# The skip term inside the Toeplitz kernel, a gate unit cut in two, and nine modulation tiles loaded ahead of the Toeplitz matrix

## The reference

```python
mod = c_silu @ w_ada + b_ada                    # six vectors of 1024: sh1 sc1 ga1 sh2 sc2 ga2
h = modulate(x, g_mix, sh1, sc1); proj = h @ w_in
u_a, z_b, gate_logits = ...                     # widths 512, 2*512 (after gelu), 2*1024
y = u * d_skip                                  # s5_mixer: the skip term
for direction in range(2):                      # complex scans over ctx, then over x
    y = y + orient(s5_readout(s5_scan(...)))
y_a = gelu(y) * sigmoid(gelu(y) @ w_glu + b_glu)
y_b = sgu_mixer(z_b, ...)
g_a, g_b = split(sigmoid(gate_logits + b_gate))
x = x + ga1 * ((g_a * (y_a @ w_proj_a) + g_b * (y_b @ w_proj_b)) @ w_out)
h2 = modulate(x, g_ffn, sh2, sc2)
x = x + ga2 * conv_ffn(h2, ...)                 # the second half of the time
```

## Time and profile before

| | |
|---|---|
| median of 3 runs | 466.66 us (465.65 to 468.84) |
| the profiled execution | 465.06 us |
| its span | 463.2 us |
| granted TensorE clock | 0.999 |
| PE busy | 447.6 us (97%) |
| DVE busy | 401.2 us (87%) |
| ACT busy | 116.5 us (25%) |
| POOL busy | 45.3 us (10%) |
| moved by DMA | 98.47 MB |

### The profile page before, as it was taken

How to read it: one execution, slowest core, us unless ns; L and a number is a source line. 1 busy time by engine, 2 the same in 40 slices (tenths; PEclk the granted TensorE clock), 3 DMA queues, 4 the chain that set the end, 5 groups by cost and what they waited for, 6 DMA issues and landing times.

```text
span 463.2 us, 7678 instructions
## 1 busy us (share of the span) xinstructions
PE 447.6 (97%) x2637; PEld 345.0 (74%) x2637; DVE 401.2 (87%) x818; ACT 116.5 (25%) x216; POOL 45.3 (10%) x73
## 2 busy tenths in 40 slices
PE   8999999989999998999999999999999999999994
PEld 5677857888888886785478888888888887444453
DVE  3599999999999867969836999999999999899744
ACT  5423355135104023201152222122122122200002
POOL 2001100002104222000000111011011011000000
PEclk9999999999999999999999999999999999999999
DMA  8994499943999999989069554554554354400002
GB/s 300 418 420 162 130 347 87 299 161 72 109 219 411 419 392 399 416 342 398 3 253 405 206 190 148 209 226 162 200 201 150 147 181 70 158 0 0 1 0 91
DMA packets 24604, 98.47 MB, mean 213 GB/s; under 512 B 7608, under 2 KB 9280, under 8 KB 16128
## 3 DMA queue, kind: packets, MB, share of 16 engines
q1 hardware_dynamic: 14592, 72.34, 44.8%
q0 software_dynamic: 5056, 18.61, 12.9%
q10 hardware_dynamic: 4928, 7.14, 4.2%
HBM read 95.49 MB, written 2.60 MB: 212 GB/s over the span
## 4 chain that ended last, share of the span: by engine, by line
PE 59%; DVE 20%; DMA 16%; POOL 2%; ACT 1%; issue 1%; DVEq 0%; SPq 0%; ACTq 0%; POOLq 0%
PE bank L756 33%; PE bank L767 14%; DVE s_region L1052 11%; DMA h_all<-mod_w 9%; PE bank L711 5%; DMA s_region<-k_scratch 5%; PE bank L667 5%; DVE s_region L1171 2%; DMA ctx_region<-ctx_t 2%; DVE s_region L1309 1%; DVE h_all L1225 1%; POOL s_region L373 1%; PE bank L482 1%; POOL s_region L383 1%; DMA k_scratch<-s_region 1%
## 5 line engine op out<-in xcount | busy, mean ns | idle before, releaser
L756 PE MATMUL bank<-h_all,s_region 128*128 128x256 f32 x704 | 152.3, 379 | 0.2 <-ACT h_all L966 0.2
L756 PEld LDWEIGHTS bank<-h_all,s_region 128*128 128x128 f32 x704 | 133.2, 190 | 19.1 <-ACT h_all L966 0.6
L1571 DVE SCALAR_TENSOR_TENSOR ctx_region<-ctx_region,pk_sb 128x189 f32<-128x189 f32 (+2 forms) x352 | 130.2, 443 | 0.3 <-DVE ctx_region L1571 0.2
L573 PE MATMUL bank<-h_all,ring_region 128*128 128x256 f32 x256 | 56.2, 380 | 0.3 <-DVE s_region L1340 0.3
L573 PEld LDWEIGHTS bank<-h_all,ring_region 128*128 128x128 f32 x256 | 48.4, 190 | 7.4 <-DVE s_region L1340 0.5
L767 PE MATMUL bank<-s_region,ring_region 128*128 128x512 f32 (+1 forms) x132 | 47.8, 522 | 0.0
L767 PEld LDWEIGHTS bank<-s_region,ring_region 128*128 128x128 f32 x132 | 25.0, 190 | 22.5 <-issue 20.3
L984 ACT ACTIVATE ctx_region<-bank 128x512 f32<-128x512 f32 x22 | 13.1, 597 | 113.3 <-PE bank L756 60.1
L1052 DVE TENSOR_TENSOR s_region<-s_region,power 128x2048 f32<-128x2048 f32 (+1 forms) x16 | 38.1, 2420 | 0.2
L396 POOL TENSOR_TENSOR ring_region<-gates,ctx_region 128x256 f32 x22 | 17.2, 784 | 178.2 <-ACT gates L992 178.2
L482 PE MATMUL bank<-h_all,ring_region 128*128 128x256 f32 x128 | 31.1, 388 | 0.2 <-ACT h_all L829 0.2
(11 more groups left out here) (242 smaller groups left out, 529.5 us busy)
## 6 DMA issues: line engine op xcount, KB each, us to landing
s_region<-up_w SPq DMA_DIRECT2D x33, 1024.0 KB, 4.9
ring_region<-ring_w SPq DMA_DIRECT2D x20, 1024.0 KB, 9.0
s_region<-mod_w POOLq DMA_DIRECT2D x20, 512.0 KB, 15.4
s_region<-early_w SPq DMA_DIRECT2D x4, 1024.0 KB, 21.8
s_region<-out_w SPq DMA_DIRECT2D x4, 1024.0 KB, 12.7
gates<-mod_w ACTq DMA_DIRECT2D x8, 512.0 KB, 5.4
gates<-early_w SPq DMA_DIRECT2D x2, 1024.0 KB, 10.8
s_region<-k_scratch POOLq DMA_DIRECT2D x8, 256.0 KB, 12.4
```

The lines of the kernel that those rows point to most:

```text
L573: mx = pe.matmul(bank[5 - j % 2][:, mm * TOK:(mm + 1) * TOK], ring[:, u % RING, (mm * KD + k) * P:(mm * KD + k + 1) * P], h_x[:, k, :], st ...
L756: mx = pe.matmul(bank[s % 3][:, half * TOK:(half + 1) * TOK], up_ring[:, s, (half * KD + k) * P:(half * KD + k + 1) * P], h2[:, k, :], sta ...
L1571: dve.scalar_tensor_tensor(out=o, in0=a, scalar=cw[:, tile[half], (dy + 1) * 3 + dx + 1], in1=o, op0=ALU.mult, op1=ALU.add).then_inc(s_con ...
```

## The change

- **Skip term.** `eye_h`, an identity of 16 by 16 repeated down the partitions, comes in with the packed parameters. DVE multiplies it by `s5_d` once (`skip_eye`, 128x64), and adds it to lag 0 of K in `k_sb` between the copies of jobs 5 and 7. The copy `u_x` (L1270) and the eight multiply-adds of L1434 are gone. ACT takes the gelu straight from the two PSUM banks, in two instructions. ACT copies job 6 before it stores K, and the store waits for the addition (`s_k_skip`).
- **POOL's queue.** `c_bc` and tiles 0 to 8 are issued as soon as their buffers are free; then come the wait for the stored K and the eight loads of `m_toep`, then tiles 9 to 23.
- **Modulation sums.** DVE makes 9 instead of 12 ahead of ga1's addition and 14 in all ahead of `y_a`, where there were 18; then three, one behind each of the merges 0 to 5, and sum 23 behind the sums of the output weights.
- **Gate unit 0** is cut in two: its first half stands where it stood, its second between chunk jobs 1 and 2.
- **Merge.** One multiplication of 128x512 stands for two of 128x256.

```diff
@@ packed parameters
-("s5_d", KS), ("conv_b", 2 * KF), ("conv_w", 2 * KF * 9)]:
+("s5_d", KS), ("conv_b", 2 * KF), ("conv_w", 2 * KF * 9), ("eye_h", H)]:
+        skip_eye = a_raw[:, 0:KS * H].rearrange("p (m h) -> p m h", m=KS)
+        k_lag0 = k_sb.rearrange("p (m j h) -> p m j h", m=KS, j=LAGS)[:, :, T - 1, :]
@@ POOL's queue
-            pool.wait_ge(s_k_out, 16)
-            for tau in range(T):
-                pool.dma_start(m_toep[tau * H:(tau + 1) * H, :, :],
-                               k_dram[:, :, (T - 1 - tau) * H:(2 * T - 1 - tau) * H].rearrange("m (g h) n -> h (m g) n", h=H)).then_inc(s_m, 16)
             pool.wait_ge(s_e_ps, 8)
-            pool.wait_ge(s_m, 16 * T)
             pool.dma_start(c_bc, c_row.partition_broadcast(P)).then_inc(s_crow, 16)
             for t in range(MT):
                 if t == S5_TILES:
                     pool.wait_ge(s_sgu_ps, 2)
+                if t == MTS:
+                    pool.wait_ge(s_k_out, 16)
+                    for tau in range(T):
+                        pool.dma_start(m_toep[tau * H:(tau + 1) * H, :, :],
+                                       k_dram[:, :, (T - 1 - tau) * H:(2 * T - 1 - tau) * H].rearrange("m (g h) n -> h (m g) n", h=H)).then_inc(s_m, 16)
                 if t >= MTS:
                     pool.wait_ge(s_mt_used, t - MTS + 1)
@@ PE
-            def gate_unit(j):
+            def gate_unit(j, halves=(0, 1)):
-                for mm in range(2):
+                for mm in halves:
-                mx.then_inc(s_unit, 1)
+                if halves[-1] == 1:
+                    mx.then_inc(s_unit, 1)
             pe.wait_ge(s_win, 16)
-            gate_unit(0)
+            gate_unit(0, (0,))
             pe.wait_ge(s_uchunk, 16 * T)
             pe.wait_ge(s_z, 2)
             for job in range(E_BANKS):
+                if job == 2:
+                    gate_unit(0, (1,))
...
-            pe.wait_ge(s_ygelu, 1)
+            pe.wait_ge(s_ygelu, 2)
...
-            pe.wait_ge(s_y, 2 * KS)
             projection(3, 0)
@@ ACT
-            act.wait_ge(s_ux, 1)
+            act.wait_ge(s_u_out, 16 * KS)
...
-            act.wait_ge(s_k, 2)
+            chunk_inputs_copied(6)
+            act.wait_ge(s_k_skip, 1)
             act.dma_start(k_dram[:].rearrange("m p n -> p m n"), k_sb[:, :].rearrange("p (m n) -> p m n", m=KS)).then_inc(s_k_out, 16)
-            chunk_inputs_copied(6)
...
-            act.wait_ge(s_y, 2 * KS)
-            act.activation(y_gelu.rearrange("p m (c t) -> p m t c", t=T), y_feat, ACT.Gelu_apprx_tanh).then_inc(s_ygelu, 1)
+            for b in range(2):
+                act.wait_ge(s_y_tr, b + 1)
+                act.activation(y_gelu.rearrange("p m (c t) -> p t m c", t=T)[:, 4 * b:4 * b + 4],
+                               bank[b][:, :].rearrange("p (t m c) -> p t m c", t=4, m=KS), ACT.Gelu_apprx_tanh).then_inc(s_ygelu, 1)
@@ DVE
-            dve.wait_ge(s_uf, KS)
-            dve.tensor_copy(u_x[:, :].rearrange("p (m c) -> p m c", c=CH), u_feat.rearrange("p m t c -> p (m t) c")[:, :, CH:2 * CH]).then_inc(s_ux, 1)
+            dve.wait_ge(s_pk2, 16)
+            tt(skip_eye, par("eye_h").unsqueeze(1).broadcast_to([P, KS, H]), par("s5_d").unsqueeze(2).broadcast_to([P, KS, H]), ALU.mult)
...
             for job in (3, 4, 5, 7):
+                if job == 7:
+                    dve.wait_ge(s_k, 2)
+                    dve.tensor_tensor(k_lag0, k_lag0, skip_eye, ALU.add).then_inc(s_k_skip, 1)
                 dve.wait_ge(s_e_ps, job + 1)
...
-            modulation_sums(0, 12)
-            dve.wait_ge(s_mt_used, 12)
+            modulation_sums(0, 9)
+            dve.wait_ge(s_mt_used, 9)
             dve.tensor_tensor(mod2[:, 0:KD], mod_sum[:, 0:KD], par("b_ada")[:, 2 * KD:3 * KD], ALU.add).then_inc(s_ga1, 1)
-            dve.wait_ge(s_pk2, 16)
-            for b in range(2):
-                dve.wait_ge(s_y_tr, b + 1)
-                y_ps = bank[b][:, :].rearrange("p (t m c) -> p m t c", t=4, m=KS)
-                for m in range(KS):
-                    dve.scalar_tensor_tensor(out=y_feat[:, m, 4 * b:4 * b + 4], in0=u_x[:, m * TOK:(m + 1) * TOK].rearrange("p (t c) -> p t c", t=T)[:, 4 * b:4 * b + 4],
-                                             scalar=par("s5_d")[:, m:m + 1], in1=y_ps[:, m], op0=ALU.mult, op1=ALU.add).then_inc(s_y, 1)
-            modulation_sums(12, 18)
+            modulation_sums(9, 14)
             for m in range(KS):
                 dve.wait_ge(s_glu, m + 1)
                 dve.tensor_tensor(y_a[:, m, :], y_gelu[:, m, :], glu_gate[:, m, :], ALU.mult).then_inc(s_ya, 1)
-            modulation_sums(18, 20)
+            modulation_sums(14, 17)
...
-                t = merge_tmp[:, 0, :], merge_tmp[:, 1, :]
-                tt(t[0], src[:, 0:TOK], gates[:, m, :], ALU.mult)
-                tt(t[1], src[:, TOK:2 * TOK], gates[:, KD + m, :], ALU.mult)
+                tt(merge_tmp, src[:, :].rearrange("p (b t) -> p b t", b=2), gates[:, m:m + KD + 1:KD, :], ALU.mult)
                 settle()
...
-                if m < MT - 20:
-                    modulation_sums(20 + m, 21 + m)
+                if m < 6:
+                    modulation_sums(17 + m, 18 + m)
...
             dve.tensor_tensor(wo12, wo22, wo12, ALU.subtract).then_inc(s_to, 1)
+            modulation_sums(23, MT)
```

More of the change, by code:

```diff
@@ L70 @@
 for _name, _w in [("c", KD), ("c_ctx", KD), ("b_ada", NMOD * KD), ("g_mix", KD), ("pick", 2), ("g_ffn", KD),
-                  ("b_gate", 2 * KD), ("b_glu", KS), ("s5_d", KS), ("conv_b", 2 * KF), ("conv_w", 2 * KF * 9)]:
+                  ("b_gate", 2 * KD), ("b_glu", KS), ("s5_d", KS), ("conv_b", 2 * KF), ("conv_w", 2 * KF * 9), ("eye_h", H)]:
     _PK[_name] = (_at, _at + _w)
@@ L114, in build @@
         y_tok = ctx_region[:, 0:1024]
-        y_feat = ctx_region[:, 1024:2048].rearrange("p (m t c) -> p m t c", m=KS, t=T)
         glu_gate = ctx_region[:, 0:1024].rearrange("p (m t) -> p m t", m=KS)
@@ L237, in build @@
         s_wsrc, s_tr, s_win = sem("w_src_ready"), sem("transposed"), sem("w_in_evacuated")
-        s_ux = sem("u_x_copied")
         s_bpad, s_ca = sem("b_pad_ready"), sem("ca_ready")
@@ L244, in build @@
         s_sgu_ps, s_yb = sem("sgu_in_psum"), sem("y_b_ready")
-        s_k_ps, s_k, s_k_out, s_m = sem("k_in_psum"), sem("k_evacuated"), sem("k_stored"), sem("m_loaded")
+        s_k_ps, s_k, s_k_skip, s_k_out, s_m = sem("k_in_psum"), sem("k_evacuated"), sem("skip_added_to_k"), sem("k_stored"), sem("m_loaded")
         s_e_ps, s_e, s_ev, s_scan = sem("e_in_psum"), sem("e_evacuated_by_act"), sem("e_evacuated_by_dve"), sem("carry_ready")
@@ L249, in build @@
         s_y8_ps, s_y8, s_y_tr = sem("y_by_chunk_in_psum"), sem("y_by_chunk_ready"), sem("y_transposed")
-        s_y, s_ygelu = sem("y_with_skip_ready"), sem("y_gelu_ready")
+        s_ygelu = sem("y_gelu_ready")
         s_glu_ps, s_glu, s_ya = sem("glu_in_psum"), sem("glu_gate_ready"), sem("y_a_ready")
@@ L1451, in _ @@
                 src = bank[PROJ_BANK[m % 4]]
-                t = merge_tmp[:, 0, :], merge_tmp[:, 1, :]
-                tt(t[0], src[:, 0:TOK], gates[:, m, :], ALU.mult)
-                tt(t[1], src[:, TOK:2 * TOK], gates[:, KD + m, :], ALU.mult)
+                tt(merge_tmp, src[:, :].rearrange("p (b t) -> p b t", b=2), gates[:, m:m + KD + 1:KD, :], ALU.mult)
                 settle()
-                dve.tensor_tensor(merged[:, m, :], t[0], t[1], ALU.add).then_inc(s_mg, 1)
+                dve.tensor_tensor(merged[:, m, :], merge_tmp[:, 0, :], merge_tmp[:, 1, :], ALU.add).then_inc(s_mg, 1)
                 dve.wait_ge(s_mg, m + 1)
-                if m < MT - 20:
-                    modulation_sums(20 + m, 21 + m)
+                if m < 6:
+                    modulation_sums(17 + m, 18 + m)
                 elif m == 6:
@@ L1746 @@
     pk = np.concatenate(_features(a["c"][0], a["c_ctx"], a["b_ada"][0], a["g_mix"][0]) + [pick]
-                        + _features(a["g_ffn"][0], a["b_gate"][0], a["s5_b_glu"][0], a["s5_d"][0], a["conv_b"][0]) + [conv_w], axis=1)
+                        + _features(a["g_ffn"][0], a["b_gate"][0], a["s5_b_glu"][0], a["s5_d"][0], a["conv_b"][0]) + [conv_w, np.tile(np.eye(H, dtype=np.float32), (P // H, 1))], axis=1)
     def per_state(v):
```

## The result

The changed kernel takes 483.49 us (median of 5, 479.25 to 485.08) against 466.66 us (also a median of 5, 465.65 to 468.84): a ratio of 1.036, with a 95% interval of 1.032 to 1.039. It is slower by 17 us, outside the range of 463.3 to 470.9, and the prediction had given "slower" a chance of 0.10, for a reason that holds only a part of this. The profiled execution took 484.69 us, its span 482.7, 19.5 us over that of before.

The account below looks back on a forecast made before the run. PE, busy for 97% of the span, was taken to set the end. Terms -0.47 (front), +4.6 (matrix), -2.26 (gelu) and -1.09 (`y_a`) gave +0.8 us, 467.4 us on the median, range 463.3 to 470.9.

Parts of the forecast that it names:

- term for the matrix: At L635, the Toeplitz product: m_toep lands at 151.2 behind nine tiles, so PE waits 4.6 us.
- When the matrix starts: On POOL's queue: tiles, K store and ring unit 13 take 16.3 us from 108.9, so the matrix starts moving at 125.2.
- If it then takes its 26.0 us again: At m_toep's loads: the matrix takes the 26.0 us from issue to landing of before, landing at 151.2.
- in both cases about two ring units are due beside it: At m_toep's loads: about two ring units are due beside the matrix before and after, supporting the 4.6 us wait.
- The lower one: Bound at L635: no ring unit beside the matrix, 17.4 us and 0.4 of latency, landed at 143.0, no wait.
- The upper one: Bound at L635: ring units 14 to 16 get in whole, 3.15 MB at 4.1 us, landed at 155.9, wait 9.3 us.
- The rival built on the rule: At L635: units 14 to 16 share the engines with the matrix throughout; wait 7.5 to 9.3 us or more, chance 0.13.
- That is hidden: Store of K: goes at about 112.0 instead of 109.11, lands within some 8 us while tiles still move; no cost.
- The front: Ahead of gate unit 1: DVE is 0.47 us earlier; the rest of the 1.28 us gap becomes a DVE wait.
- The gelu and `y_a`: Waits ahead of L688 and the last projections go whole: -2.26 us for the gelu, -1.09 us for `y_a`.
- the sum of these terms: Front, gelu and `y_a` together: the change gives 3.8 us if the matrix causes no wait.
- Sum 23: In DVE's idle 1.60 us ahead of 221.53: hidden, though SP's first L756 loads move from about 202 to 217.

Follow-up runs that it names:

- matrix-first run: Changed kernel with POOL's queue as before: stored K and the eight matrix loads, then the wait for them, then c_bc and tiles; 466.65 us, ratio 1.003.
- the fillers: Changed kernel with 36 dummy matmuls of 256 columns ahead of PE's wait for the matrix; 480.11 us, ratio 1.031.
- the run with the order alone: Kernel before with only POOL's queue reordered, c_bc and nine tiles ahead of the Toeplitz matrix; 479.52 us, ratio 1.030.
- the run with gate unit 0 whole: Changed kernel with matrix first, no wait behind it, skip term ahead of job 3's copy, and gate unit 0 in one piece; 461.03 us, ratio 0.991.
- the early skip term: Changed kernel with POOL's queue as before and the skip term added ahead of DVE's copy of job 3, not job 7; 461.56 us, ratio 0.995.

## Why the prediction was wrong

**The place was right, the size not.** The prediction named L635 as the point where the change is decided, and a wait for `k_scratch` there as the new largest wait. Its term for the matrix was +4.6 us with bounds of 0 and 9.3; measured were 16.7. In the span the forecast was +0.8 and the result +19.5; of the 18.7 us between them 12.1 are this wait and 6.5 what PE lost behind it (2.7 to the end of gate unit 6, 1.1 in the carry run, 2.7 in gate unit 7).

- *When the matrix starts.* It was to start at 125.2, behind 16.3 us of other bytes. POOL issued the eight loads at 125.26, which agrees by luck: the store of K took 13.2 us among the tiles, not "some 8". And the bytes ahead were not through by then. They were priced at 416 GB/s from a stretch in which 1.15 of 1.25 MB were the ring's and not tiles'; in the changed kernel the four stretches of 4 us from 108 on had 105, 305, 405 and 425 GB/s, and the 6.8 MB that the prediction counts (5.24, 0.49 and 1.05) had moved only at about 129. This is some 4 of the 12 us by which the matrix landed later than forecast.
- *How long it takes.* "If it then takes its 26.0 us again" is the step that failed, and "in both cases about two ring units are due beside it", its reason. It was 37.8 us from issue to landing, from 125.3 to 163.0. The 26.0 us of before hold about 14 us in which the matrix had the engines alone and moved 1.4 to 1.9 times as fast as it did beside the ring. Moved by 12 us it lost these, and 4.35 MB of ring units 13 (its end), 14, 15, 16 and 17 moved beside it. Holding back units 16 and 17 gave 6.7 us back.
- *The bounds.* The lower one took the 17.4 us of engine time as the matrix's own cost. The matrix-first run shows 12.1 us for the same bytes, and alone, at 0.40 to 0.45 MB in four microseconds, 2.10 MB would need some 19 to 21 us (an estimate). Its 0.4 us of latency stands in no row. The upper one counted the three units due until the expected landing, at 4.1 us a MB. Unit 17, issued at the end of gate unit 5 (which is unit 13: the load of a unit waits for the unit four before it, not three), came in as well, at 5.0 us a MB. The rows of before had the better price: 0.23 MB in four microseconds beside the ring is 36 us for 2.10 MB (an estimate), 161 us when counted from 125.2 and 165 from 129. The last load landed at 163.0.

**The round-robin rule.** The prediction set aside the Trainium skill's rule ("DMA: Bandwidth & Descriptors", Queues, rings and completion order: each DMA engine takes a packet from each queue row with work in turn) for one row of before, in which q0 had 102%. While both had work, the changed kernel agrees with turns: from 134 to 156 us q0 had 465 packets and q1 417. The trace of before does not agree in its first part, where ring unit 13 was issued at 119.7 and q1 had no packet until 128; why, no run here tells. The rival built on the rule had the mechanism right, and ended at 472 us because it had the same bound of three units and no clock in it.

**The clock was missing.** No term or rival had it. A wait of 16.7 us was followed by the 1.2 GHz level, and PE lost 2.7 us on its next two pieces of work, as the fillers show by giving them back; some 2.7 us more went in gate unit 7 behind the 1.20 us gap. The five profiled kernels with waits of 4.4, 9.9, 14.8, 16.0 and 16.7 us at the Toeplitz product all ran its 64 records in 3.64 us; with 2.4 us they took 1.95. The trace of before had the clock at 1.00 everywhere and could not give the price, but it could have been named: PE had never stood still for over 2.3 us in it, and the forecast was that it would.

**"That is hidden", of the late store of K.** It was nearly true in the changed kernel (up to 3 us, by the run with the order alone) and only there. The prediction costed it against the tiles ahead of the matrix. With the matrix first, the 2.6 us became 10.7 us of landing and 2.4 us of wait, and together with the later tiles took all of the 3.8 us that the other edits had won.

**What held.** The front: gate unit 1 starts 0.63 us earlier (0.47 forecast), and the removed issue gap turned into a wait for DVE, 0.79 us in place of 0.25; the run with gate unit 0 whole gives the same time. The gelu and `y_a`: the changed kernel is no evidence here, since its late PE would have hidden both waits without any edit, as the order alone shows. But they are gone as well in every run with these edits whose matrix was in time: with the early skip term L691 starts 2.3 us earlier than the front accounts for, and the output products 1.4 us more. With the matrix out of the way, the sum of these terms, -3.8 us, is what the kernel with the early skip term shows: -4.3 us in the span, -4.0 in the medians. Sum 23 behind the output sums was costed at nothing; in the changed kernel a wait of 0.6 us for a `w_up` load stands in the down projection. It does not follow from that edit alone: the run with the order alone has 0.4 us of it without the edit, and the runs with the early skip term have the edit and no such wait.

## What to carry to other kernels

A transfer that is moved behind others is not only shifted by their bytes: ask what will move beside it in its new place, and take its pace from a stretch of the trace in which the same queues are busy together. A mean over a time that it had partly to itself, or its share of the engines, does not carry over; here the pace beside the ring was a half to three quarters of that alone. When a forecast has PE stand still for longer than it ever did in the trace, add the slower clock behind the wait as a term of its own, even if the trace can only tell that it is unknown. And an instruction that stands behind the wrong neighbour in an in-order queue can cost over fifteen times itself: here 0.2 us of DVE, three copies late, made a difference of 5 us by the medians (466.65 and 461.56) and of 3.5 by the ratios (1.003 and 0.995).

## What the runs showed of the hardware

- Behind each wait of 4.4 us or more PE's granted clock was 0.50, the 1.2 GHz level, and it came back to 1.00 some 3.6 to 5.7 us after PE went on. Behind the waits of 2.4 and 2.5 us for the matrix it stayed at 1.00. The product of 64 records of 128x128 took 3.64 in place of 1.95 us.
- Matmuls on 64 rows run at 27 to 30 ns a record, 256 records in a row, came to a stop of 0.7 to 2.5 us for no wait of the program in nearly every kernel. Work put in between moves the stop (1.28 us, in the next unit) or, with four dummy matmuls (2.0 us) in the changed kernel, makes it vanish from the trace. Each stop ended 2.2 to 2.6 us after a 16 KB packet of the instruction queue q8 began.
- With the engines full, loads in runs of 512 bytes to 16 partitions moved 0.40 to 0.45 MB in 4 us alone and 0.23 to 0.31 MB beside SP's 1 MB loads, which moved 0.57 to 0.65 MB in the same time. The engine time charged to the same 2.10 MB was 17.4 us in one kernel and 12.1 in another.
- A ring load issued while only the matrix was moving had no packet for over 8 us (issued at 119.7, none until 128) and landed after 18.2; among the tiles it landed after 7.9.
